# Cross attention's query weights stay in their place until expert 219 and are loaded once, and experts 14 to 131 have one gather slot fewer

## The reference, cut to what matters

```
def memory_attention(xn, mem_k, mem_v, w_cq, w_co):
    q = (xn @ w_cq)...            # w_cq is 1024 x 256: 1 MB
    ...softmax(q k) v... @ w_co
def block(xt):                    # 128 tokens
    ...top 16 of 128 x 128 keys for each of 8 heads -> idx, gate
    h = einsum('td,thkd->thk', xt, u_tab[idx])
    a = gelu(h) * gate
    return einsum('thk,thkd->td', a, v_tab[idx])
```

## Time and profile before

| | us |
|---|---|
| median of 3 runs | 1700.69 (1700.62 to 1706.0) |
| profiled execution, its own time | 1698.98 |
| its span | 1697.2 |
| PE busy | 1305.5 (77%) |
| DVE busy | 1165.7 (69%) |
| ACT busy | 807.3 (48%) |
| POOL busy | 640.6 (38%) |
| moved by DMA | 657.88 MB, mean 388 GB/s |

### The profile page before, as it was taken

One profiled execution on the slowest core, in us unless ns is written; L12 is line 12 of the kernel. 1 busy time (PEld: TensorE's weight loads), 2 busy tenths in 40 slices (PEclk: granted clock), 3 DMA queues, 4 the chain that ended last, 5 costly groups with the idle time before them and its releaser, 6 DMA issues.

```text
span 1697.2 us, 21662 instructions
## 1 busy us (share of the span) xinstructions
PE 1305.5 (77%) x7069; PEld 474.1 (28%) x7069; DVE 1165.7 (69%) x2798; ACT 807.3 (48%) x2337; POOL 640.6 (38%) x584
## 2 busy tenths in 40 slices
PE   9998987878888677677777776777677777677665
PEld 4454442433344222133222111212112111111110
DVE  2545749797667676777777677777666677677764
ACT  1424456784434454455555444445444445444443
POOL 0000234434434334444444443444444444443441
PEclk9999998989999888889988877878878777878876
DMA  9426799999999999999999999999999999999995
GB/s 358 167 100 251 276 386 419 405 369 421 421 420 421 420 390 401 421 401 420 422 420 419 421 421 422 421 422 422 420 421 422 421 410 421 422 421 420 422 417 232
DMA packets 97441, 657.88 MB, mean 388 GB/s; under 512 B 12512, under 2 KB 15584, under 8 KB 20768
## 3 DMA queue, kind: packets, MB, share of 16 engines
q0 software_dynamic: 83056, 604.28, 86.3%
q1 hardware_dynamic: 14272, 52.21, 8.0%
HBM read 653.24 MB, written 4.19 MB: 387 GB/s over the span
## 4 chain that ended last, share of the span: by engine, by line
DMA 44%; PE 24%; DVE 12%; ACT 10%; issue 7%; POOL 2%; ACTq 0%; DVEq 0%; SPq 0%; POOLq 0%
DMA R<-in_peer_uv,R 42%; PE ps L2115 9%; PE ps L1622 5%; DVE R L1541 4%; PE ps L1862 3%; ACT L952 2%; POOL R L682 2%; ACT R L961 2%; PE ps L1593 1%; ACT R L956 1%; ACT R L952 1%; ACT L860 1%; DVE R L1329 1%; DVE R L1330 1%; DVE R L1332 1%
## 5 line engine op out<-in xcount | busy, mean ns | idle before, releaser
L2115 PE MATMUL ps<-R 64*64 64x512 f32 x4528 | 735.6, 730 | 356.6 <-ACT R L961 347.3
L682 POOL DMA_INDIRECT R<-in_peer_uv,R x566 | 627.0, 1108 | 849.8 <-PE ps L2115 774.2
L1541 DVE CUSTOM_DVE_ANT_0 R<-R 128x1024 f32<-128x1024 f32 x566 | 688.0, 1225 | 376.0 <-DMA R<-in_peer_uv,R 367.6
L952 ACT ACTIVATE R<-R 128x1 f32<-128x1 f32 x576 | 115.8, 201 | 609.4 <-DVE R L1541 596.7
L2115 PEld LDWEIGHTS ps<-R 64*64 64x64 f32 x4528 | 134.9, 149 | 708.2 <-ACT R L961 606.9
L961 ACT ACTIVATE R<-R 128x64 f32<-128x64 f32 x576 | 200.4, 348 | 54.9 <-ACT R L956 1.9
L1862 PE MATMUL ps<-A,R 128*128 128x256 f32 (+1 forms) x640 | 222.9, 471 | 1.3 <-ACT R L837 0.7
L956 ACT ACTIVATE R<-R 128x1 f32<-128x1 f32 x576 | 169.8, 295 | 20.8
L1862 PEld LDWEIGHTS ps<-A,R 128*128 128x128 f32 (+1 forms) x640 | 95.5, 199 | 260.5 <-issue 257.0
L1622 PE MATMUL ps<-A,R 128*128 128x512 f32 (+1 forms) x256 | 101.2, 545 | 0.4 <-ACT R L733 0.4
L1593 PE MATMUL ps<-R 128*128 128x256 f32 (+2 forms) x352 | 81.2, 387 | 0.0
(11 more groups left out here) (304 smaller groups left out, 946.6 us busy)
## 6 DMA issues: line engine op xcount, KB each, us to landing
R<-in_peer_uv,R POOLq DMA_INDIRECT x566
A<-in_w_pq SPq DMA_DIRECT2D x8, 1024.0 KB, 7.9
A<-in_w_in SPq DMA_DIRECT2D x3, 2048.0 KB, 20.3
R<-in_w_out SPq DMA_DIRECT2D x5, 1024.0 KB
x_res<-in_x_prompt SPq DMA_DIRECT2D x6, 512.0 KB, 12.3
R<-in_w_out SPq DMA_DIRECT2D x1, 3072.0 KB
R<-in_x_promptT SPq DMA_DIRECT2D x4, 512.0 KB, 8.7
R<-in_w_cq SPq DMA_DIRECT2D x2, 1024.0 KB, 10.6
```

The costliest lines, as they stand in the source:

```text
L682: pool.indirect_dma_start(slots[slot_of[g]], None, I["peer_uv"][:, :], bass.IndirectOffsetOnAxis(ap=idx[:, b % 4, k:k + 1], axis=0)).then_ ...
L952: act.activation(hgelu[:, b % 2, col], hdot[:, b % 2, col], ACT.Gelu).then_inc(gelu_ready, 1)
L1541: dve.tensor_tensor_reduce(u, u, xn(t), 1.0, 0.0, ALU.mult, ALU.add, hdot[:, b % 2, k:k + 1]).then_inc(u_used, 1)
L2115: ins = pe.matmul(bank(2 * (t % 2) + q)[rows], diag[tokens, g % DIAGS, :], v_rows[slot_of[g]][tokens, c * 512:(c + 1) * 512], start=first, ...
```

## The change

The second copy of the query weights and its load are gone, and with it PE's wait for it; all tiles use the first copy, in slot 5's region. Slot 5 therefore leaves the rotation until expert 225 and slot 6, free after output piece 11, takes its place from expert 132. POOL's first-use waits change with it: slot 6 waits for the 12 output pieces, slot 5 for tile 4's query product. The distance to the holder becomes 5 for experts 14 to 17, 6 for 19 to 30, 7 for 32 to 78, 6 for 79 to 131, 7 for 133 to 139, and is as before from 140 on. The last expert of slot 9 becomes 71 instead of 66, so L605 waits for `v_used` 72 instead of 67; the last of slot 7 before the reload of `w_co` stays 134.

```diff
-SLOT_PHASES = ((0, (9, 8)), (2, (1, 2, 3, 4, 9, 8)), (8, (1, 2, 3, 4, 9)), (14, (3, 4, 9, 1, 2, 5)),
-               (18, (0, 9, 1, 2, 3, 4, 5)), (31, (0, 1, 2, 3, 4, 5, 7, 9)), (74, (0, 1, 2, 3, 4, 5, 7)), (140, (0, 1, 2, 3, 4, 5)), (225, (0, 1, 2, 3, 4, 5, 6)), (278, tuple(range(9))))
+SLOT_PHASES = ((0, (9, 8)), (2, (1, 2, 3, 4, 9, 8)), (8, (1, 2, 3, 4, 9)), 
+               (18, (0, 9, 1, 2, 3, 4)), (31, (0, 1, 2, 3, 4, 7, 9)), (74, (0, 1, 2, 3, 4, 7)),
+               (132, (0, 1, 2, 3, 4, 6, 7)), (140, (0, 1, 2, 3, 4, 6)), (225, (0, 1, 2, 3, 4, 5, 6)), (278, tuple(range(9))))
...
-        w_cq2 = v3(R[:, 20480:22528], KD)
...
-            sp.wait_ge(o_mm, 12)
-            load(w_cq2, v3(I["w_cq"][:, :], KD), ld_wcq)
...
                     elif slot_of[g] == 5:
-                        pool.wait_ge(p_q, 2)
+                        pool.wait_ge(p_q, TILES)
                     elif slot_of[g] == 6:
-                        pool.wait_ge(p_q, TILES)
+                        pool.wait_ge(o_mm, len(OUT_AT))
...
                         pe.wait_ge(p_T, t + 2)
-                        if t == 2:
-                            pe.wait_ge(ld_wcq, 32)
-                    w = w_cq if t == 1 else w_cq2
...
-                    ins = product(out, lambda k: w[:, k, c * P:(c + 1) * P], lambda k: xT[:, k, :])
+                    ins = product(out, lambda k: w_cq[:, k, c * P:(c + 1) * P], lambda k: xT[:, k, :])
```

## The result

The changed kernel is slower: median 1708.88 us of 22 runs (1704.64 to 1717.57) against 1703.12 us of 22 runs of the kernel before (1697.92 to 1709.68), ratio **1.0039, 95% interval 1.003 to 1.0048**, which is 6.6 us (the medians alone are 5.8 us apart; from here on a cost in us is worked out from the ratio). The forecast was 1700.4 (1696.7 to 1706.7) and "no change"; the measured time lies above the range, in the case that had 0.15. The kernel before measured 2.4 us slower in these runs than in the three that the forecast started from; the ratio put on those, 1707.3, lies above the range too. The profiled execution has a span of 1705.5 against 1697.2.

The account below looks back on a forecast made before the run. The kernel was taken as a loop around one full DMA pipe, 2.49 us per 1.05 MB gather. The terms -2.49 +1.2 +0.7 +0.3 gave -0.3 us, so 1700.4 us against the median 1700.69, range 1696.7 to 1706.7.

Parts of the forecast that it names:

- the case that had 0.15: Whole kernel slower by over 0.3%, above 1705.8 us: chance 0.15, made of 0.08 for rival (a) and 0.07 for Rival (b).
- part 1: Removed second load of the query weights, issued at 547.25 us into a full pipe: gain of 1.05 MB, -2.49 us.
- Part 2: Gathers 14 to 17, five slots instead of six: issues 4.50 and 3.93 us later, cost +1.2 us (0 to 2.5).
- Part 3: Experts 18 to 131, one slot fewer: only gather 74 falls short, +0.7 us (bounds 0 to 3).
- the rule for the slack: Slack of gather g: landing of g-1 plus 2.49, minus its issue plus 5.58; loss only where it was under 2.49 us.
- above 2.49: Experts 18 to 131: all slacks besides those of gathers 39, 64 and 74 exceed 2.49 us, so nothing is lost there.
- an unloaded latency of 6.6: Experts 18 to 131, if cover were 1 us thinner: gather 39 would be 1 us short and 74 1.7.
- each slack shrinks by 2.49 us: Steady state, one slot fewer: a gather waits for the expert one later, finished 2.49 us later.
- Part 4: SP's queue: x_prompt's reload 10.6 us later, output weights behind it, PE waits some 2 us at expert 77; +0.3 us (0 to 3).
- rival (a): Output piece 0 starved: loads get a quarter of the pipe, PE waits 11 us instead of 2, total 1709; chance 0.08.
- Rival (b): Lost slot costs a whole gather, 2.49 us, at each of 14, 39, 74 and 84: 10.0 in all, total 1708; chance 0.07.

Follow-up runs that it names:

- experiment 9: The kernel before, with the second load of w_cq cut to the first of its eight parts: 1698.70 us, ratio 0.9985.
- experiment 4: The changed kernel with the load of w_cq and TensorE's wait for it put back: 1711.79 us, ratio 1.0053 to the kernel before.
- "rest" run: The kernel before, POOL waiting one expert longer for gathers 18 to 131 except 22 issued just ahead of a gap: 1704.47 us, ratio 1.0019.

## Why the prediction was wrong

**Right: what bounds the kernel, and part 1.** The load was worth about what its bytes take in a full pipe: -2.49 us forecast for 1.05 MB, -2.6 (0.9 to 4.1) measured for 0.92 MB. That it "hid behind nothing" holds. The choice against the fixed cost of about 2 us for each DMA, which the Trainium skill (DMA: Bandwidth & Descriptors, section "Anatomy of one DMA") gives for the path of the gathers and which would have made it -4.5 by an estimate from that page, rests on the 2.49 us from landing to landing. No run here tests it alone: experiment 9 keeps the load, and experiment 4's 2.4 us is uncertain by 2.9. The distances from 140 on are those of before, and from there the two traces run side by side.

**Part 2, right in its mechanism, its size open.** The issue of gather 14 moved just as forecast. The price was put at the middle of 0 and 2.5; the ratios give 2.4, the medians 0.5, and the traces 0.4 and 0.7 by expert 20. Which it is the record does not say.

**Part 3, the main error: +0.7 forecast, +5.4 measured** (uncertain by 3). The step that failed is the rule for the slack: that a gather is covered if it is issued 3.09 us (5.58 less 2.49) before the landing of the one before it. Gather 45, issued 4.74 to 5.26 us before it, still came 0.85 to 1.08 us late. So the slacks listed as "above 2.49" were not safe, and all over the stretch gathers lost time that the sum had at nothing; the "rest" run alone, gathers without a stall behind them, costs 3.2 us. The 5.58 us itself was right: 5.7 for gather 64 and 6.14 for 83, in the middle of the stretch. The doubt about "an unloaded latency of 6.6" looked for the weakness there, in the latency, and not in the rule.

There is a second slip, "each slack shrinks by 2.49 us": true on average, but a gather that was issued just ahead of a stall of the experts on PE comes just behind it, 6.2 us later for gather 44. Part 2 moves each gather to the issue time of the next, and part 3 uses the mean. By itself this slip cost nothing. With each gather of 18 to 131 moved to the old issue time of the next and the rule left as it is, only 73 falls short by 0.68 us and 38 by 0.01 (worked out from the rows of the kernel before, 63 left out), which is the forecast's 0.7 again. How the loss splits over single gathers stays open: two executions of nearly the same code differ by 2 us and more in this stretch (the changed kernel and two variants of it had fallen back by 3.8, 6.2 and 2.6 us between experts 8 and 72), which no single trace can resolve.

**Part 4, mechanism right, size wrong in two directions.** The place, the order and x_prompt's new issue were right: 10.6 us later forecast, and 404.51 less the 5.6 us of delay by then is 398.9. PE's wait was put at some 2 us (412.4 less 410.83 is 1.6) and was 9.79. Two terms make up the rest. The two loads took 17.9 us from the first issue to the landing instead of 13.5, 4.4 us more, since SP got 36% of the bytes over the 14 us and not half; it had got the same 36% in the kernel before, and the 4 us of the earlier trace rows were too little to set the share. And 3.8 us are the missing slot's: expert 71, which lets the loads go, was 5.6 us late, while PE came to output piece 0 only 1.8 us late. It is rival (a), nearly word for word (11 us of wait), but from two causes. What (a) adds, "to the end nearly whole", was wrong: taking the 9.79 us away gave some 1 us back beside the missing slot, and a wait of 10.47 us with all slots cost 2.7. I think that queued gathers and landed ones that DVE had not yet used covered the rest; that was not tried.

**The rivals.** Rival (b), the slot costs at every narrow place, was the nearest, at 0.07. Its reason, a spread between DMA engines, agrees with the completion events. Its sum of 10.0 is near the 7.8 of parts 2 and 3 together, but the places differ (44 to 64, and 84 to 100, not 39 and 74), so the nearness is in part luck. The argument against it was that DVE paces the stretch since its waits at 41 and 73 are short. A short wait of DVE can as well mean that the landing was only just late, and so that there was no cover left.

## What to carry to other kernels

Where a ring of buffers feeds a full pipe, price a missing buffer by how long before the landing of its forerunner a transfer must be issued, and read that lead from places in the same stretch where two landings are further apart than the period. The latency in an empty pipe gave 3.09 us here, and 4.74 to 5.26 were not enough. The bytes of a load in a full pipe are worth their time: here 2.6 us for 0.92 MB, against some 5 for the buffer given up for it.

## What the runs showed of the hardware that was not expected

A gather into a nearly empty pipe landed 5.58 us after its issue early in the kernel, and 5.7 (gather 64) and 6.14 us (83) after it in the middle of the changed kernel. The gather right behind it, issued 1.44 and 1.55 us later, landed 3.50 and 3.33 us behind it, where the full pipe has 2.49. At expert 45 the landings stood over 3.3 us apart in six of the kernels, though 45 had been issued 3.5 to 5.3 us before 44 landed; at expert 203, in four kernels, a lead of 3.0 to 4.0 us lost less than 0.2 us. What makes the difference was not tried. The 16 completion events of one gather were 1.9 us apart in the median of 240 to 560 us in the changed kernel. SyncE's queue, with two loads of 1.05 MB beside the gathers, got 36% of the bytes over 14 us in both kernels, but 56% and 34% in single windows of 4 us. And a wait of 10 us of TensorE, on the chain that ended last, was worth 1 to 3 us at the end.
